# Delta heads: order of the u and w products of one head on TensorE

## The reference, cut to what matters

```
tmat = eye + beta * (k k^T) * dec_strict
sol  = triangular_solve(tmat, concat([(beta*gam) * k, beta * v]))
wk, uv = sol[..., :DK], sol[..., DK:]
step:  u = uv - wk @ s
       o = gam * (q @ s) + a_qk @ u
       s = gend * s + k_dec^T @ u
```

## Time and profile before

| what | value |
|---|---|
| median of 3 runs | 4347.91 us (4345.66 to 4356.43) |
| profiled execution, its own time | 4334.81 us |
| its span, first to last instruction | 4333.0 us |
| mean granted clock of TensorE | 0.881 of full speed |
| TensorE matmul (PE) busy | 3461.8 us, 80% |
| TensorE weight load (PEld) busy | 2149.6 us, 50% |
| VectorE (DVE) busy | 1619.9 us, 37% |
| ScalarE (ACT) busy | 1070.0 us, 25% |
| GpSimd (POOL) busy | 866.4 us, 20% |

### The profile page before, as it was taken

One profiled execution on the slowest core, in us unless ns is written; L12 is line 12 of the kernel. 1 busy time (PEld: TensorE's weight loads), 2 busy tenths in 40 slices (PEclk: granted clock), 3 DMA queues, 4 the chain that ended last, 5 costly groups with the idle time before them and its releaser, 6 DMA issues. The chain is left out here.

```text
span 4333.0 us, 71718 instructions
## 1 busy us (share of the span) xinstructions
PE 3461.8 (80%) x28798; PEld 2149.6 (50%) x28798; DVE 1619.9 (37%) x2578; ACT 1070.0 (25%) x1606; POOL 866.4 (20%) x1037
## 2 busy tenths in 40 slices
PE   6568787879797978869444445999999799999997
PEld 2136464647475655644344443554545355555554
DVE  1224443444444443442799994223111211111112
ACT  0324243342424242422111110332111421111112
POOL 0001010100000000100877770111111111111110
PEclk8779888889898988878677777999999899999998
DMA  6210000000000000031111112321121111111111
GB/s 246 91 30 16 5 27 20 12 20 12 20 12 20 11 21 12 19 80 50 27 25 26 25 26 84 101 66 34 44 82 29 29 44 39 39 39 39 39 36 56
DMA packets 224844, 179.10 MB, mean 41 GB/s; under 512 B 24277, under 2 KB 211750, under 8 KB 222310
## 3 DMA queue, kind: packets, MB, share of 16 engines
q1 hardware_dynamic: 218358, 153.69, 12.2%
q10 hardware_dynamic: 4608, 11.54, 0.7%
q0 software_dynamic: 1648, 10.54, 0.7%
HBM read 144.20 MB, written 27.33 MB: 40 GB/s over the span
## 5 line engine op out<-in xcount | busy, mean ns | idle before, releaser
L173 POOL TENSOR_TENSOR w_pair<-w_raw,w_pair 128x1024 bf16<-128x1024 f32 (+1 forms) x156 | 348.4, 2236 | 2371.8 <-ACT w_pair L168 2371.8
L184 PE MATMUL m_out<-hn,w_pair 128*128 128x512 bf16 (+1 forms) x3168 | 573.0, 344 | 32.5 <-PEq L154 32.5
L184 PE MATMUL bank<-hn,w_pair 128*128 128x512 bf16 (+1 forms) x2304 | 498.0, 366 | 89.9 <-ACTq L1112 71.8
L184 PEld LDWEIGHTS m_out<-hn,w_pair 128*128 128x128 bf16 x3168 | 310.3, 98 | 294.9 <-issue 34.5
L184 PEld LDWEIGHTS bank<-hn,w_pair 128*128 128x128 bf16 x2304 | 217.5, 103 | 318.8 <-issue 143.1
L184 PE MATMUL m_out<-ys,w_pair 128*128 128x512 bf16 (+1 forms) x1584 | 290.4, 347 | 15.1 <-DVE ys L2005 15.1
L168 ACT ACTIVATE w_pair<-w_raw 128x1024 bf16<-128x1024 f32 x156 | 162.9, 1050 | 411.5 <-PE m_out L184 254.2
L1697 PE MATMUL s_banks<-u_block,m_block 128*128 128x160 f32 x128 | 39.9, 404 | 254.0 <-DVEq L1803 254.0
L184 PEld LDWEIGHTS m_out<-ys,w_pair 128*128 128x128 bf16 x1584 | 155.9, 99 | 149.6 <-issue 21.1
L184 PE MATMUL b_out<-ys,w_pair 128*128 128x512 bf16 (+1 forms) x1152 | 210.8, 345 | 4.0 <-PEq L1251 4.0
L2001 DVE TENSOR_TENSOR m_a<-m_out,m_sg 128x1280 f32<-128x1280 f32 x22 | 32.8, 1492 | 483.7 <-PE m_out L184 483.7
(11 more groups left out here) (330 smaller groups left out, 5647.6 us busy)
## 6 DMA issues: line engine op xcount, KB each, us to landing
w_raw<-in_w_in SPq DMA_DIRECT2D x56, 512.0 KB, 4.1
w_ada_rows<-in_w_ada SPq DMA_DIRECT2D x16, 1536.0 KB, 6.3
w_raw<-in_w_gu SPq DMA_DIRECT2D x44, 512.0 KB, 3.8
w_raw<-in_w_down SPq DMA_DIRECT2D x16, 512.0 KB, 3.8
scratch_x<-x_t POOLq DMA_DIRECT2D x1, 5120.0 KB, 16.1
scratch_o<-o_pair ACTq DMA_DIRECT2D x8, 640.0 KB, 3.7
scratch_u<-u_rows ACTq DMA_DIRECT2D x8, 640.0 KB, 3.0
u_block<-scratch_u SPq DMA_DIRECT2D x128, 40.0 KB, 1.8
```

The source lines that it names most:

```text
L173: pool.tensor_tensor(K.w_pair[:, slot, 1, 0:kt, :], K.w_raw[:, slot, 0:kt, :], K.w_pair[:, slot, 0, 0:kt, :], ALU.subtract).then_inc(K.w_l ...
L184: mm = pe.matmul(out[:, c0:c0 + cn], K.w_pair[:, slot, w, k, :], x[:, a, k, c0:c0 + cn], start=i < 3, stop=i >= 9 * kt - 3)
```

## The change

On TensorE the 5 groups of u and the 3 groups of w of a head, which ran as u0 u1 u2 u3 u4 w0 w1 w2, run as w0 u0 u1 w1 u2 u3 w2 u4. The products, their banks and their numbers in the rings stay; so does the order on every other engine. Each group of w gets a wait of its own (`rs.taken`) for the copy of its `gk`, which the order before had through the wait of the last group of u.

```
-                    for g in range(NG):
-                        rd.taken(pe, h, last_of(LEVELS - 1, of8(4 * g)))
-                        b = quad(rs.to_write(pe, h, S_UV + g, S_KT + 2 * g + 1))
-                        pe.sem_inc(K.pulse, 1)
-                        for t in range(4):
-                            for r in HALVES:
-                                mm = pe.matmul(b[r, t, :], xti[r, 4 * g + t, :], vt[r, 4 * g + t, :], start=True, stop=True)
-                        mm.then_inc(rs.full, 1)
-                    for g, (t0, n) in enumerate(G8):
+                    for what, g in (("wk", 0), ("uv", 0), ("uv", 1), ("wk", 1), ("uv", 2), ("uv", 3), ("wk", 2), ("uv", 4)):
+                        if what == "uv":
+                            rd.taken(pe, h, last_of(LEVELS - 1, of8(4 * g)))
+                            b = quad(rs.to_write(pe, h, S_UV + g, S_KT + 2 * g + 1))
+                            pe.sem_inc(K.pulse, 1)
+                            for t in range(4):
+                                for r in HALVES:
+                                    mm = pe.matmul(b[r, t, :], xti[r, 4 * g + t, :], vt[r, 4 * g + t, :], start=True, stop=True)
+                            mm.then_inc(rs.full, 1)
+                            continue
+                        t0, n = G8[g]
+                        rs.taken(pe, h, S_KT + 2 * ((t0 + n) // 4 - 1))
                         rd.to_write(pe, h, D_WK + 2 * g + 1)
                         pe.sem_inc(K.pulse, 1)
                         b = [octo(rd.bank(D_WK + 2 * g + d)) for d in range(2)]
```

## The result

The changed kernel takes 4298.54 us (median of 4 runs, 4295.62 to 4304.33), the kernel before 4349.38 us (median of 4, 4345.66 to 4356.43). The ratio is 0.9883, with a 95% interval of 0.9866 to 0.9900: 50.8 us less. The forecast was 4303, with a range of 4292 to 4329.

The account below looks back on a forecast made before the run. TensorE bounds the kernel, with stops for copies in the u and w stage and a fallen clock. Savings of 32.3 (stage), 11.4 (steps 0) and 1.1 (last head) sum to 44.8: 4347.9 - 44.8 = 4303 us, range 4292 to 4329.

Parts of the forecast that it names:

- The first group waits longer: Start of the u and w stage: w0 needs the second subtraction, so it loads 0.62 us after where u0 stood.
- Products: Weight loads in the u and w stage: five groups of u take 4.33 us, 80 of w take 4.65.
- Switches: Six changes of weight shape from w0 to the scan: 0.17 us pause each, 1.02 a head.
- the 10.62: Forecast us per head for the u and w stage: 0.62 + 4.33 + 4.65 + 1.02; over eight heads saves 32.3.
- rival B: Each change of weight shape drains the array: six at 0.44 us, 13 us more, so 4316; chance 0.10.
- Waits for copies: Before w1, u2, the scan and its step 1: all copies covered, margins 0.2 to 1.7 us; an uncovered stop costs about 1.0.
- Rival C: Other waits replace the old ones, such as slower copies, so TensorE stops as often as before: 4348; chance 0.06.
- The scan's start: Step 0 at 2.4 GHz takes 3.07 us, saving 11.4 over seven heads; the last head's first steps save 1.1.
- What moves with it: Later GpSimd edge zeroing, next head's projections and SyncE loads: nothing waits for them, and the saving is passed on.
- the clock would hold: TensorE's clock does not fall to 1.2 GHz in the u and w stage, so scan step 0 runs at 2.4 GHz.
- Rival A: Clock falls all the same in the same share of the stage; only stops are saved, 21.2 us, so 4327; chance 0.18.
- D: The wait before w0 and the switches throw TensorE to 1.2 GHz: stage 17.3 us, slower at 4369; chance 0.04.

## Why the prediction was right

1. *The first group waits longer.* Forecast 0.62, measured 426.02 - 425.41 = 0.61.
2. *Products.* Taken at 4.33 and 4.65; the loads of the changed kernel add up to 4.29 for u and 4.72 for w.
3. *Switches.* This term was sized wrong. I took 0.17 for all six. From u to w, and from u to the scan, it is 0.17, but from w to u the next load follows after 427.98 - 427.91 = 0.07 with no pause shown, so the six are 0.7 rather than 1.02 a head. That is 0.3 less, and the stage came out 0.27 under the 10.62. The pauses of the loads hide that both directions cost about the same. The first matmul of u starts at 427.99 and that of w at 429.88, each 0.06 to 0.07 before the last one of the other shape ends (426.05 + 2.00 and 427.99 + 1.96). A matmul lasts 0.27, so it starts some 0.2 after that one; inside a group one starts every 0.06. The difference, near 0.15, is what each of the four added switches cost. The Trainium skill, TensorEngine Tiling (Array Packing), Key Properties, says that a change of mode drains the TensorE. The rows come near to that, since the new shape begins just before the old one ends, but not at the price of rival B: its 0.44 added a whole matmul to a pause that already held most of this wait. In the earlier trace rows the matmuls of u end at 429.36, 0.07 after the first load of w.
4. *Waits for copies.* All were covered. At the scan, where the margin was the smallest named (0.2), some 0.1 was left. Where the cover was taken away, with w2 last, the stop of 1.0 that was named came back. Rival C fell.
5. *The scan's start.* 11.4 forecast for seven steps 0, 12.8 measured: step 5 of the scan, from which I took the time, has a wait for ScalarE that step 0 has not. Its first load of the projections comes 1.46 after the first load of the step (at 458.76), in step 0 of the changed kernel 1.25 after it (at 435.76). Here is first step 5 of before, then step 0 of the changed kernel:

```profile
460.22 0.87 PEld L184 LDWEIGHTS bank<-hn,w_pair 128*128 128x128 bf16 x6 [0.33 <-ACT kq L1021]
```

```profile
437.01 1.20 PEld L184 LDWEIGHTS bank<-hn,w_pair 128*128 128x128 bf16 x8
```

The last head's 1.1 for three steps was 1.2, but I took three steps for the whole: over its scan 0.4 was left in the first pair of profiles, and 10 us came in the second.
6. *What moves with it.* GpSimd's memsets came later, and steps 1 to 5 took no longer for it (133.4 us in seven heads before, 133.0 after).

The sum was 44.8 us, the two pairs of traces give 47.7 and 59.3, and the runs 50.8 (43.5 to 58.3 from the interval). Against the first pair the stages are 2.2 us better than forecast, the steps 0 1.4 better and the last head 0.7 worse. That 4303 and 4298.54 lie so close is in part luck, since runs of one kernel differ by about 10 us; the stretches are the better test, and they bear out the mechanism. That the clock would hold was the step with the least support. It held in 16 of 16 heads of the two profiles of the changed kernel, and had fallen in 16 of 16 before. Rival A, by which it falls anyway, and D, by which it falls at once, did not occur: the stop of 0.52 before w0 lowered it in none of the 16. What was said against A, that the pauses left are short, is what the filled stops support: with the old order and its waits, but with the stops filled wholly or to 0.3 us, the clock held in 15 of 16 stages.

Why the clock fell in some heads and not in others with the same stops (three of seven steps 0 with the stop before the scan, five of eight stages with four stops) stays open. Neither the number of stops, nor their sum, nor the place of one of them tells these heads apart, and no run here shows the rule.

## What to carry to other kernels

Where two products of one stage are emptied by two different engines, alternate their groups, so that each copy runs under the other product; sum the cover of each copy beforehand, and start with the group whose input is ready first. Count a stop of TensorE twice, once for its length and once for what the work behind it takes at 1.2 GHz: here each was about half of the gain. Before changing an order for the sake of the clock, idle products in the stops are a cheap way to learn what the clock alone is worth.

## What was not expected of the hardware

Adding 0.75 us of unused products to each of four stops made the kernel 26.5 us faster. In the order of before, with four stops of about 1.0 us in each stage, the granted clock fell in every head of both profiles. And one change between the 64x128 and the 64x64 shape of weights cost 0.15 us on the average of both directions, more than two of these matmuls take at their usual spacing of 0.06.
